# A decoder layer step on one core: identity products on TensorE in its rests at the borders of stages and in the routing

## What is computed

```
h = rms_norm(x, g_mix);  qd, kd, vd, qs, ks, vs = split(h @ w_in)           # width 3072
od = diff_attention(qd, kd, vd)      # 4 heads, two softmaxes each, w = p0 - lam * p1, head norm
os = stick_breaking(qs, ks, vs)      # 8 heads, product of sigmoids from the right
x  = x + concat(od, os) @ w_out
h2 = rms_norm(x, g_ffn)
gates = top-1 of 4 groups, then top-2 of 4 experts                          # routing
x  = x + sum_e gates * (silu(h2 @ w_gate[e]) * (h2 @ w_up[e])) @ w_down[e]  # 16 experts of width 256
y  = rms_norm(x, g_final)            # and the new k and v rows are put out
```

## Time and profile before

| | us |
|---|---|
| median of 3 runs | 1535.22 (1534.84 to 1536.3) |
| the profiled execution's own time | 1531.82 |
| its span, first to last instruction | 1530.0 |
| PE busy (share of the span) | 1331.6 (87%) |
| DVE, ACT, POOL busy | 794.0, 664.8, 146.9 |
| mean granted PE clock | 0.944 |

### The profile page before, as it was taken

The page is one execution under the profiler, slowest core; times in us unless marked ns, Lnnn a source line. Parts: engine busy times, 40 slices in busy tenths (PEclk is TensorE's granted clock), DMA queues, the critical chain, the costliest instruction groups (busy, mean ns, idle before and its releaser), DMA issues. The chain is left out here.

```text
span 1530.0 us, 26141 instructions
## 1 busy us (share of the span) xinstructions
PE 1331.6 (87%) x8895; PEld 958.5 (63%) x8895; DVE 794.0 (52%) x1078; ACT 664.8 (43%) x1078; POOL 146.9 (10%) x175
## 2 busy tenths in 40 slices
PE   7999999997798979778999898699849999999940
PEld 6877888885565556445656565488626667666620
DVE  4321122103556555547777687644365666666637
ACT  5410222012555556536555555423225566556512
POOL 1000000000000000000000000000011222222025
PEclk9999999998999989989999999899959999999975
DMA  5632433175686868657688795354277997632277
GB/s 199 200 93 73 126 109 96 52 236 188 222 286 232 297 217 288 210 173 235 241 271 293 250 324 196 108 168 162 97 268 277 406 412 277 215 121 101 83 283 258
DMA packets 159645, 319.14 MB, mean 209 GB/s; under 512 B 21816, under 2 KB 50907, under 8 KB 155419
## 3 DMA queue, kind: packets, MB, share of 16 engines
q1 hardware_dynamic: 146666, 274.48, 52.6%
q0 software_dynamic: 7200, 26.22, 5.0%
q10 hardware_dynamic: 5648, 16.78, 2.7%
HBM read 318.79 MB, written 55.77 MB: 245 GB/s over the span
## 5 line engine op out<-in xcount | busy, mean ns | idle before, releaser
L2384 DVE TENSOR_TENSOR w_gate_up_split<-w_gate_up,w_gate_up_split 128x2048 fp32r<-128x2048 f32 x64 | 143.8, 2289 | 110.0 <-ACT w_gate_up_split L2433 109.4
L2335 PE MATMUL gate_up_ps<-w_gate_up_split,slot_rows_T 128*128 128x512 f32 x768 | 186.1, 398 | 3.6 <-DVE slot_rows_T L2392 3.3
L325 PE MATMUL proj_ps<-w_in_split,x_T_hi 128*128 128x512 f32 x576 | 186.2, 399 | 0.0
L2335 PEld LDWEIGHTS gate_up_ps<-w_gate_up_split,slot_rows_T 128*128 128x128 f32 x768 | 143.3, 190 | 39.4 <-DVE slot_rows_T L2392 10.3
L1176 PE MATMUL turns_and_scores_ps<-ident,pages 128*128 128x128 f32 (+1 forms) x1088 | 147.6, 281 | 17.6 <-DVE sample_rest_products L1435 5.3
L1176 PEld LDWEIGHTS turns_and_scores_ps<-ident,pages 128*128 128x128 f32 (+1 forms) x1088 | 122.8, 146 | 53.3 <-issue 52.7
L2433 ACT ACTIVATE w_gate_up_split<-w_gate_up 128x2048 fp32r x62 | 115.3, 1908 | 34.0 <-issue 34.0
L325 PEld LDWEIGHTS proj_ps<-w_in_split,x_T_hi 128*128 128x128 f32 x576 | 109.2, 190 | 26.1
L459 ACT ACTIVATE proj_rows<-proj_ps,sum_squares 128x512 f32<-128x512 f32 x36 | 24.8, 688 | 230.5 <-PE proj_ps L325 230.5
L2357 PE MATMUL expert_out_ps<-w_down,expert_act_T 128*128 x256 | 115.2, 593 | 1.3 <-ACT expert_out L2463 1.3
L325 PE MATMUL proj_ps<-w_in_split,x_T_lo 128*128 128x512 f32 x288 | 114.9, 399 | 0.0
(11 more groups left out here) (229 smaller groups left out, 1926.8 us busy)
## 6 DMA issues: line engine op xcount, KB each, us to landing
pages<-in_cache_s SPq DMA_DIRECT2D x256, 256.0 KB, 4.3
pages<-in_cache_d SPq DMA_DIRECT2D x226, 256.0 KB, 4.4
w_gate_up<-in_w_gate SPq DMA_DIRECT2D x34, 1024.0 KB, 8.2
w_gate_up<-in_w_up SPq DMA_DIRECT2D x34, 1024.0 KB, 10.1
w_down<-in_w_down SPq DMA_DIRECT2D x34, 1024.0 KB, 12.2
scratch_moe_out<-expert_out ACTq DMA_DIRECT2D x32, 512.0 KB, 4.2
w_in_now<-in_w_in SPq DMA_DIRECT2D x48, 256.0 KB, 2.9
pages_ahead<-in_cache_d SPq DMA_DIRECT2D x30, 256.0 KB, 3.5
```

What stands on the lines that cost most here:

```text
L325: last = pe.matmul(pj_ps[:, n % PJ_BANKS, :], h[:, k, at], w[g % 2][:, k, :], start=(k == 0 and m == 0), stop=(k == KC - 1 and m == 2))
L2335: last = pe.matmul(gu_ps[:, u, :], xT[:, u, a, k, :], gu_split[:, u, b, k, :], start=(k == 0 and m == 0), stop=(k == KC - 1 and m == 2))
L2384: dve.tensor_tensor(gu_split[:, u, 1, at, :].rearrange("p k (c n) -> p k c n", c=2), raw[:, at, :, :], gu_split[:, u, 0, at, :].bitcast(F3 ...
```

## The change

A helper issues fp32 products of the constant identity matrix with itself (128x128 times 128x128) into a given place in PSUM; nobody reads them. It is called at ten points with fixed counts: at the end of project (behind a wait for the last kT copy, since it writes that bank); in the first score step of DIFF, into the ring place of that very score, for which the wait for the place now stands ahead of the wait for q and k; at the start of either attention block, ahead of the wait for zeroed; at the end of DIFF, behind a wait for the last o_kept; at the start of mix_out; at the start of route, behind its counts and at its end, into a PSUM bank of its own; and at the start of experts. No semaphore is signalled by them, and no other engine's program changes.

```diff
+def keep_running(pe, t, into, times):
+    for _ in range(times):
+        pe.matmul(into, t.ident[:, :], t.ident[:, :], start=True, stop=True)
...
+                pe.wait_ge(tr_kept, len(turned))
+                keep_running(pe, t, tr_ps[:, 0, 0:P], BORDER_RUNS["projected"])
...
+BORDER_RUNS = {"projected": 10, "first_heads": 13, "first_kind": 4, "first_kind_end": 17, "second_kind": 2, "mixing": 26, "routing": 21,
+               "counted": 23, "placed": 11, "gathered": 24}
...
                 def score(it, i, g):
+                    place_free(pe, "score", it, i, g)
+                    if kind == DIFF and (it, i, g) == (0, 0, 0):
+                        keep_running(pe, t, ring[places["score", it, i, g]][:, 0, 0:P], BORDER_RUNS["first_heads"])
                     if g == 0:
                         pe.wait_ge(t.qk_loaded[it % 2], 32 * ((it + TURNS * kind) // 2) + 32)
-                    place_free(pe, "score", it, i, g)
...
+                if kind == DIFF:
+                    keep_running(pe, t, o_ps[:, 0:P], BORDER_RUNS["first_kind"])
+                else:
+                    keep_running(pe, t, o_ps[:, 0:P], BORDER_RUNS["second_kind"])
                 pe.wait_ge(zeroed, 1)
                 for name, *args in plan:
                     if name in steps:
                         steps[name](*args)
+                if kind == DIFF:
+                    pe.wait_ge(o_kept.sem, o_kept.after(TURNS - 1, PT - 1))
+                    keep_running(pe, t, o_ps[:, 0:P], BORDER_RUNS["first_kind_end"])
...
+                keep_running(pe, t, y_ps[:, 0, 0:P], BORDER_RUNS["mixing"])
                 for n in range(TILES):
                     product(n, 0)
...
+        idle_ps = ctx.enter_context(nc.psum_tensor("kept_running_ps", [P, BANK], F32))
...
+                keep_running(pe, t, idle_ps[:, 0:P], BORDER_RUNS["routing"])
                 pe.wait_ge(step, t.n_member)
...
                 pe.matmul(cnt_ps[:, 1, 0:TILES * E], t.before[:, :], member[:, :, :], start=True, stop=True)\
                   .then_inc(counted, 1)
+                keep_running(pe, t, idle_ps[:, 0:P], BORDER_RUNS["counted"])
...
                 pe.matmul(tok_ps[:, 0:COL_TILE], lanes[:, :], t.sums_of_parts[:, :], start=True, stop=True)\
                   .then_inc(placed, 1)
+                keep_running(pe, t, idle_ps[:, 0:P], BORDER_RUNS["placed"])
...
+                keep_running(pe, t, y_ps[:, 0, 0:P], BORDER_RUNS["gathered"])
+
                 def turn_rows(tile):
```

## The result

| | before | after |
|---|---|---|
| median, us (11 runs each) | 1534.84 (1532.1 to 1536.3) | 1540.89 (1537.3 to 1544.4) |
| ratio, 95% interval | | 1.0035 [1.0020, 1.0051] |
| span of the profiled execution | 1530.0 | 1539.2 |
| mean granted PE clock | 0.944 | 0.954 |

The account below looks back on a forecast made before the run. PE was taken as busy 1331.6 of 1530.0 us, with only awaited work at 1.2 GHz winnable. Terms +3.9 - 0.6 - 0.25 - 0.3 - 2.9 gave -0.15 us, so 1535.1 on the median; range 1530.8 to 1539.0.

Parts of the forecast that it names:

- first_heads, the delay: DIFF's first score: 13 products start only after DVE's page copy, delaying the score 5.1 us; bounds 2.9 and 5.6.
- first_heads, what comes back: Behind DIFF's first score: PE's 4.4 us of slow work runs fast, giving back 1.2 us, at most 2.2.
- gathered: Experts' start: 24 products fit ahead of the gathered rows; transposes and gate_up then run faster, -2.9 us; bounds 0, 3.1.
- second rival: Clock falls between routing's and experts' batches; gate_up slow again, 2.3 of 2.9 us lost; sum +2.35; chance 0.18.
- DIFF's border: DIFF's end and next attention start: 17 and 2 products, later barrier against faster transposes and scores; -0.6 us.
- mixing: mix_out's start: 26 products end before oT_split comes; PE then follows DVE's splits more closely; -0.25 us.
- Routing, counts, placed: Routing: batches of 21, 23 and 11; first late by 0.1 us, counts give back 0.4; sum -0.3 us.
- The base: Whole kernel: profiled execution's own 1531.8 us, median 3.4 above it; the difference of -0.15 put on the median, 1535.1.
- Rival 1: First score: its rest gets filled, so the 13 products cost about 0; -4.0, 1531.2 us; chance 0.22.
- Rival 3: All batches: products hold no clock, each takes double, nothing comes back; +15, 1550 us; chance 0.04.

Follow-up runs that it names:

- second repeat: The kernel before, unchanged, profiled once more, the second of three such looks: 1533.58 us, span 1531.8, mean clock 0.941.
- filled_first: The changed kernel with 26 products instead of 13, in the free o_ps bank ahead of the first score's wait for the place: 1534.85 us, ratio 1.0009 against before.
- repeats 1 and 3: The kernel before, unchanged, profiled once more each, first and third of three such looks: 1532.16 and 1530.83 us, mean clock 0.943 in both.
- thin_kept: The kernel before with only routing's and experts' batches, resized and with products in the thin stretches, waits in old order: 1530.3 us, ratio 0.9975.
- thin_filled: The kernel before with only routing's and experts' batches, resized and with products in the thin stretches, waits in the change's order: ratio 0.9995 against before.
- order_only: The kernel before with only the new order of the two waits ahead of each score, no products: 1532.0 us, ratio 0.9981.

## Why the prediction was wrong

The prediction had 1535.1, and at most 1539.0; 1540.89 was measured. The mechanism of the loss was the right one and its price was too low; what was to pay for it mostly didn't come. Two terms failed: what comes back behind the thirteen (1.2 us foretold, 0.7 more lost) and the gain at the experts' start (2.9 foretold, 0.1 in the trace after; all nine other batches 4.05 foretold, none measured). Against the second repeat of the kernel before, which like it has no fall in project and has the further one in DIFF (at 442 us, at 449 after), the profile after is 7.4 us longer (1539.2 less 1531.8): 5.5 up to the first score, 0.7 up to the first turned tile, 0.9 from there to the thirty-first, -0.3 at DIFF's border, -0.5 in the routing, -0.1 at the experts' start, 0.9 behind the last matmul (where no product was added, and the traces here lie between 57.6 and 59.9 us), and the rest within 0.15 a stretch.

- **first_heads, the delay: 5.1 foretold, 5.5 measured.** By the second repeat's trace; 5.4 from the row of the batch to that of the score. Both bounds held. The rest was ended by DVE's page copy, as said, and q and k were long there.
- **first_heads, what comes back: the first step that failed.** I took 1.2 us back in the first turns, "at most half, 2.2". It came, and was lost at once. Measured from the first score, the first weight transpose stands 3.8 us behind it (371.35 to 375.15) and 5.7 before (368.19 to 373.90): 1.9 back. But the sample scores behind it wait for ACT's copy of a page and come only 0.7 us earlier (6.66 us behind the score, 7.37 in the second repeat), and then run at half clock, because of the fall at 377.6:

```profile
373.06 1.07 PE L1193 MATMUL turns_and_scores_ps<-k_pages_T,q_by_block 128*32 128x256 f32 x16 [1.19 <-ACT k_pages_T L1507]
...
374.07 1.09 PE L1176 MATMUL turns_and_scores_ps<-ident,pages 128*128 128x128 f32 x8
```

These two, of the second repeat, took 1.07 and 1.09 us; after, they took 1.94 and 1.64. In place of 1.2 back there is 0.7 more. I had asked what the faster work gives its followers, and not whether the clock would stay up through the stretch behind it, which is thin (PE 4.67 of 6.80 us) and thinner for being done fast. That its thinness takes the clock down is argued: no run filled it. Nor was 1.2 to be had with the clock up: filled_first keeps it at 1.00 throughout and its first tile comes 0.5 us earlier. The net of this term was to be +3.9, at most +4.4. It is +6.2 by the traces. The upper bound was built wrong as well: it took the 1.2 as certain, and 5.6 with nothing back would have been the bound.
- **The rest of DIFF, +0.9: not foreseen.** It is there by the fourth turned tile: at 412 us the clock is down for 6.8 us, 3.4 in the second repeat (repeats 1 and 3 have the long one too). All three profiles with the thirteen have the further fall of the clock at 449 us, but so have nine of the fifteen without them, at 442 to 445. Of the executions with the thirteen alone, all 11 are of the slower group; of the kernel before, 48 of 80. From these two shares, a shift from 60% to all adds 0.4 x 3.1 = 1.3 us to a mean. That is a count over 11 executions and three traces. In the changed kernel as a whole both groups occur (five runs at 0.956 or more, median 1538.4, six at 0.954 or less, median 1542.4), so there it isn't shown.
- **gathered, -2.9: the second step that failed; right in size, wrong in how often.** Given where the clock stays up (10.8 to 10.9 us in five traces), -0.1 in the trace after, where it fell in front of gate_up. With 2.8 us this is the largest miss of a term. This is the second rival's mechanism, which had 0.18, and of which the prediction named the place (the stretch with the transposes alone) and the price (2.3 of the 2.9). It came in four of five profiles with the counts of the change: wholly in after, and with some 1.5 us of the 2.9 lost in the three others. With six products more between the transposes and gate_up it came in none of three.
- **DIFF's border, -0.6: -0.3 by the traces; mixing, -0.25: 0.** The next block begins 0.55 us later (DVE's memset stands 5.42 us behind the last turned tile, 4.87 in the second repeat), its first transposes are 2.0 faster, and 1.1 of this is lost again before STICK's first turned tile: the clock is at 0.51 from 695.2 to 702.0. The same miss as at the first score. In mix_out PE follows DVE's splits, as said.
- **Routing, counts, placed, -0.3: -0.5.** The counts began 0.1 late and were fast; small as foretold.
- **The base.** The prediction put the difference on the median of before, 3.4 us above the profiled execution. Right in form; but the profiled execution was one without the fall at 442, and of the 80 six in ten are of the other group. One sum is off: the top of rival 2, +3.7 on this base, is 1538.9 and not 1538.5; the range of up to 1539.0 held it.

Rival 1, that the rest at the score gets filled, is what filled_first built: with the products ahead of the wait they cost and give nothing that can be measured (place in the program and PSUM bank changed together, as they must). The prediction gave it 0.22 although its own rows (the releaser is what the products wait for) spoke against it; the chance belonged on the side of the loss. Rival 3 fell: the products do hold the clock.

**What may beat both kernels.** thin_kept, the routing's products in the filled form with the old order of waits, has 0.9975 [0.9958, 0.9992] against before, 1530.3 beside 1534.64. But thin_filled, the same products on another chip, had 0.9995, and against order_only, on the same chip, thin_kept is 1.7 us faster. Each of their traces has the 2.9 us at the experts' start; a gain of 1 to 3 us in the median is possible, and it isn't shown beyond the spread between kernels with equal work.

## What to carry to other kernels

Products that keep TensorE's clock up cost nothing measurable here where they fit into the rest: into a place in PSUM that is free anyway, ahead of the wait that ends the rest. Behind that wait they are work on the path, at half clock, just when the clock is down. And they can pay only if the clock is still up when the long work comes: look at the thin stretch between the batch and that work, not at the batch. Even then, 2.9 us in a trace gave medians of 0.9997, 0.9995, 0.9995 and 0.9975 of before here. Ahead of trusting a difference of 0.2%, look at how executions of one and the same kernel spread with their mean clock, and compare group with group.

## What the runs showed of the hardware

- Transposes alone raise the clock: 48 of them at the experts' start, 0.50 in their first 3 us, 0.94 in the stretch behind.
- The clock falls at other moments in other executions of the same kernel, with the same work on PE: with or without one at 442 us (profiles with it are 3 us longer through DIFF, 1.6 of it lost there), with or without one at 93 us (2.4 us longer, 1.4 to 1.6 of it there). Times of the kernel before spread over 1529 to 1537, apart from two at 1540 and 1542, and it sat mostly in one group on one chip (21 of 26) and about evenly on two others (27 of 54).
- A mean clock higher by 0.010 is no shorter time when idle stretches were filled: 1539.2 us at 0.954, 1530.0 us at 0.944.
- The clock at which the work behind a filled rest runs need not be worth much: 0.5 us in filled_first, with 1.00 from project's end to beyond the first turned tile.
- What stays open: why five products in the rest of the first score, which delay it by 2.4 us, put five of seven timed executions 6 us up.
